# An encoder block whose experts' weights stream from memory: 1 MB parts in 16 recurring slots, in place of 2 MB halves in 8 recurring and 3 single-use slots

## The chip, the cores and the metric

The program runs on one core of one Trainium2 chip. The core has TensorE (PE; its weight loads are shown as PEld), VectorE (DVE), ScalarE (ACT), GpSimd (POOL) and SyncE (SP), and 16 DMA engines that move data between the chip's memory and SBUF. TensorE writes its products into the eight banks of PSUM. The metric is the device time of one execution in microseconds (us); lower is better.

## The reference

One encoder layer for x of 512 tokens by 1024 features, float32:

```python
h = rms_norm(x, norm1_g)                       # input projection, two attention branches, gates
x = x + einsum(gate_a * ya + gate_b * yb, w_out)
x = x + expert_choice_swiglu(rms_norm(x, norm2_g), w_router, w_gate, w_up, w_down)
return rms_norm(x, normf_g)

def expert_choice_swiglu(h, w_router, w_gate, w_up, w_down):
    aff = softmax(h @ w_router)                # 16 experts
    g, idx = top_k(aff.T, cap)                 # each expert takes its cap = 64 best tokens
    xin = h[idx]
    y = (silu(xin @ w_gate) * (xin @ w_up)) @ w_down * g
    return zeros.at[idx].add(y)
```

Each expert has three matrices of 1024 by 1024, 4 MB each: 16 experts have 192 MB, and each byte of them is read once.

## The kernel before, in words

The 512 tokens lie as four tiles of 128 (index c). The attention, the gates and the output projection come first. Then each tile's x2 is turned and multiplied with the router matrix, while the last output projections still run on TensorE; VectorE finds each expert's 64 tokens in eight rounds of "the best eight, then strike them out" (L1628, L1631), counts them (`count`), and forms `pos`, each token's place in its expert. `keep_clock` puts unused products on TensorE where it waits.

From `pos` a 0/1 matrix picks tokens. The experts go in eight pairs. For a pair, `gather` multiplies `pick` with the normalised rows of x2, held as a high part `xn_hi` and the rest `xn_lo` (both in the format fp32r), which gives the 2 x 64 chosen rows; `turn_xin` turns them so that features are on partitions, and VectorE applies the gain norm2_g (`xinT`). `gate_up(p, e)` multiplies them with the gate and up matrices of expert e of pair p. ScalarE applies the sigmoid, VectorE the two products (`activate`), `turn_act` turns the result into `actT`, and `down(p)` multiplies it with the down matrices. `y_hi` and `y_lo` are y times the token's affinity in two parts; `scatter` brings them back to the tokens through `give`, the turned `pick`, in four pieces between the products of the next pair's first expert, and VectorE adds them to x2 (`add`). After the last pair comes the final norm. Before the last down products TensorE copies x2 of three tiles into PSUM (L1338), to which the last pieces are added.

The first pair is gathered another way, since its xn parts are not there yet: `pick_first` holds the picks times the norm factor, and `gather_first` multiplies x2 itself with it, in full fp32 (which TensorE runs as two rows per product in the trace), so that the result is already turned. Its second half stands between the first expert's products. The parts `xn_hi` and `xn_lo` are made inside pair 0, once the slots whose memory they take are used.

The weights come through SyncE's queue in halves of 2 MB, 12 a pair: gate and up of expert 0 (h = 0, 1), of expert 1, and then the down halves in the order (h 0: e 0, e 1), (h 1: e 0, e 1). `slot_of` gives the slot: eight slots recur, and halves 3, 4 and 7 have a slot of their own that is used once. Eleven halves are loaded before the first gate product, some during the gates and the output projection, the last four after it. Then each load waits until the half that held its slot is used (`w_slot_used`); the first two of them are cut in two parts (`w_part_used`). The queue is in order. Engines work through their own programs in order too, and wait on semaphores.

## Time and profile before

| | us |
|---|---|
| median of three runs (lowest, highest) | 939.11 (937.24, 940.04) |
| the profiled execution, its own time | 939.72 |
| its span, from the first to the last instruction | 937.9 |
| busy: TensorE products, weight loads | 880.4, 564.7 |
| busy: VectorE, ScalarE, GpSimd | 350.2, 246.9, 21.8 |

In the profile "busy" is the time in which at least one instruction of the engine was running. A product of 128x512 in fp32 is two rows of the table, each 596 ns long and overlapping its neighbours. "DMA share" is the mean busy share of the 16 DMA engines; it can read a little above 1. "[0.75 <-PE psum L1109]" means that the engine was idle for 0.75 us before the instruction, and that this wait was ended by TensorE's line 1109.

### The profile page before, as it was taken

What the parts mean: (1) busy time and instruction counts of PE and PEld (TensorE: products, weight loads), DVE (VectorE), ACT (ScalarE), POOL (GpSimd) and SP (SyncE); (2) the same over time, 40 slices, a digit from 0 to 9 for tenths busy, and PEclk for the clock granted to TensorE, in tenths of its full rate; (3) what the DMA queues carried; (4) which work ended last, traced back from release to release, by engine and by line L of the source; (5) the groups of instructions that cost most, each with busy time, mean ns of one, the idle gap of its engine ahead of it and who ended that gap; (6) DMA issues with size and microseconds to landing.
All of it is one profiled execution on the core that took longest, in us unless ns stands there. A gap on an engine that the chain in (4) does not pass through costs nothing.

```text
span 937.9 us, 11252 instructions
## 1 busy us (share of the span) xinstructions
PE 880.4 (94%) x4730; PEld 564.7 (60%) x4730; DVE 350.2 (37%) x606; ACT 246.9 (26%) x445; POOL 21.8 (2%) x42
## 2 busy tenths in 40 slices
PE   5999899799989999899999999999998998989985
PEld 5999766578768888899954343343433434334332
DVE  4368676665714434333613221213121121221203
ACT  4433766665633322222002001010100101001002
POOL 1040000000000000000000000000000000000001
PEclk7999999999999999999999999999999999999999
DMA  8433111302127623772665899999999999999992
GB/s 262 96 91 90 45 45 46 112 18 63 51 71 226 196 80 106 266 273 88 273 237 211 346 428 428 427 427 429 427 427 426 430 428 426 430 427 426 428 419 101
DMA packets 77921, 239.78 MB, mean 256 GB/s; under 512 B 7728, under 2 KB 63152, under 8 KB 65072
## 3 DMA queue, kind: packets, MB, share of 16 engines
q1 hardware_dynamic: 72304, 235.94, 63.9%
q10 hardware_dynamic: 5568, 3.13, 1.2%
q8 instruction: 38, 0.62, 0.3%
q14 instruction: 11, 0.09, 0.0%
HBM read 236.96 MB, written 2.10 MB: 255 GB/s over the span
## 4 chain that ended last, share of the span: by engine, by line
PE 77%; DMA 16%; DVE 3%; ACT 2%; issue 1%; POOL 0%; SPq 0%; DVEq 0%; ACTq 0%
PE psum L1238 18%; DMA wslot<-in_w_down 14%; PE psum L863 10%; PE psum L865 10%; PE psum L864 10%; PE psum L1272 9%; PE psum L1292 3%; PE psum L1000 2%; PE psum L1012 2%; PE psum L1187 2%; PE psum L1199 2%; PE psum L869 2%; DMA w_raw<-in_w_in 1%; PE psum L970 1%; PE psum L986 1%
## 5 line engine op out<-in xcount | busy, mean ns | idle before, releaser
L1238 PE MATMUL psum<-wslot,xinT 128*64 128x512 f32 x1024 | 230.5, 596 | 11.5 <-DMA wslot<-in_w_up 6.1
L1238 PEld LDWEIGHTS psum<-wslot,xinT 128*64 128x64 f32 x1024 | 71.5, 137 | 152.5 <-issue 138.2
L1272 PE MATMUL psum<-wslot,actT 128*64 128x512 f32 x512 | 112.6, 594 | 7.7 <-DMA wslot<-in_w_down 7.7
L1379 DVE TENSOR_TENSOR w_lo<-w_raw,w_hi 128x1024 fp32r<-128x1024 f32 (+1 forms) x56 | 65.1, 1185 | 74.7 <-ACT w_hi L575 74.3
L863 PE MATMUL psum<-hT_hi,w_hi 128*128 128x512 f32 x224 | 88.9, 397 | 1.4 <-DVE qB_next L1477 1.4
L865 PE MATMUL psum<-hT_hi,w_lo 128*128 128x512 f32 x224 | 87.5, 391 | 0.0
L864 PE MATMUL psum<-hT_lo,w_hi 128*128 128x512 f32 x224 | 87.4, 390 | 0.0
L1272 PEld LDWEIGHTS psum<-wslot,actT 128*64 128x64 f32 x512 | 37.7, 137 | 77.5 <-issue 76.3
L813 ACT ACTIVATE act<-psum 128x512 f32<-128x512 f32 x16 | 9.6, 597 | 234.2 <-PE psum L1238 234.2
L575 ACT ACTIVATE w_hi<-w_raw 128x1024 fp32r<-128x1024 f32 (+1 forms) x56 | 55.7, 1021 | 26.0 <-DMA w_raw<-in_w_out 12.4
L1710 DVE TENSOR_TENSOR x<-x,psum 128x512 f32<-128x512 f32 x56 | 36.0, 684 | 67.5 <-PE psum L1292 67.5
L1694 DVE SCALAR_TENSOR_TENSOR y_lo<-psum,slot_aff,y_hi 128x512 fp32r<-128x512 f32 x16 | 11.3, 746 | 126.7 <-ACT y_hi L828 126.7
L863 PE MATMUL psum<-w_hi,hT_hi 128*128 128x256 f32 x192 | 55.8, 291 | 2.2 <-DVE w_lo L1379 2.2
L864 PE MATMUL psum<-w_lo,hT_hi 128*128 128x256 f32 x192 | 55.4, 288 | 0.0
L865 PE MATMUL psum<-w_hi,hT_lo 128*128 128x256 f32 x192 | 55.4, 288 | 0.0
L863 PEld LDWEIGHTS psum<-hT_hi,w_hi 128*128 128x128 f32 x224 | 42.1, 188 | 12.1 <-issue 3.9
L865 PEld LDWEIGHTS psum<-hT_hi,w_lo 128*128 128x128 f32 x224 | 42.1, 188 | 9.1
L864 PEld LDWEIGHTS psum<-hT_lo,w_hi 128*128 128x128 f32 x224 | 42.1, 188 | 8.3
L828 ACT ACTIVATE y_hi<-psum,slot_aff 128x512 fp32r<-128x512 f32 x16 | 10.1, 685 | 127.7 <-PE psum L1272 127.7
L1685 DVE TENSOR_TENSOR act<-act,psum 128x512 f32<-128x512 f32 x16 | 10.9, 684 | 86.0 <-ACT act L813 86.0
L863 PEld LDWEIGHTS psum<-w_hi,hT_hi 128*128 128x128 f32 x192 | 37.9, 197 | 2.6 <-issue 2.6
L863 PE MATMUL psum<-w_hi,mT_hi 128*128 128x256 f32 x128 | 36.7, 287 | 2.5 <-DVE x L1564 1.5
(190 smaller groups left out, 1260.1 us busy)
## 6 DMA issues: line engine op xcount, KB each, us to landing
wslot<-in_w_up SPq DMA_DIRECT2D x32, 2048.0 KB, 28.7
wslot<-in_w_gate SPq DMA_DIRECT2D x31, 2048.0 KB, 26.4
wslot<-in_w_down SPq DMA_DIRECT2D x31, 2048.0 KB, 32.7
w_raw<-in_w_in SPq DMA_DIRECT2D x40, 512.0 KB, 4.6
w_raw<-in_w_out SPq DMA_DIRECT2D x8, 512.0 KB, 8.0
x_in<-in_x SPq DMA_DIRECT2D x4, 512.0 KB, 10.3
w_raw<-in_w_o_a SPq DMA_DIRECT2D x8, 256.0 KB, 2.8
x<-in_x SPq DMA_DIRECT2D x1, 2048.0 KB, 7.9
```

The source lines that it names most:

```text
L575: act_.activation(hi, raw, ACT.Copy).then_inc(w_hi_done, 1)
L863: pe.matmul(out_, s_hi, m_hi, start=(k == 0), stop=False)
L864: pe.matmul(out_, s_hi, m_lo, start=False, stop=False)
L865: return pe.matmul(out_, s_lo, m_hi, start=False, stop=(k == n_k - 1))
L869: pe.matmul(into[:, 0:P], ident[:, :], ident[:, :], start=True, stop=True)
L1000: t = pe.transpose(tp[(0, 3)[u % 2]][:, P * k:P * k + P], probs_of(u)[:, P * k:P * k + P], ident[:, :])
L1012: mm = pe.matmul(tp[2][HD * hh:HD * hh + HD, :], vA[:, k, HD * kv:HD * kv + HD], pT[:, hh, k, :], start=(k == 0), stop=(k == NT - 1))
L1238: mm = pe.matmul(bank[2 * e + n][CAP * f:CAP * f + CAP, :], xinT[:, HALF * h + k, CAP * e:CAP * e + CAP], wslot[slot][:, k, SEQ * f:SEQ * ...
L1272: mm = pe.matmul(bank[4 + f][CAP * e:CAP * e + CAP, :], actT[:, e, k, CAP * h:CAP * h + CAP], wslot[slot][:, k, SEQ * f:SEQ * f + SEQ], st ...
L1292: mm = pe.matmul(bank[6 + f][:, :], give[:, p % 2, P * c:P * c + P], part[:, SEQ * f:SEQ * f + SEQ], start=(part is y_hi), stop=(part is y ...
L1379: dve.tensor_tensor(lo, raw, hi.bitcast(F32), ALU.subtract).then_inc(w_split, 1)
L1710: dve.tensor_tensor(part, part, bank[6 + f][:, :], ALU.add).then_inc(added, 1)
```

## The change

- Slots. Every half is now two parts of 1 MB (half of each partition's 16 KB). Part m goes to slot m mod 16; no slot is used once. 16 parts are loaded before the first gate product. The memory of the slots that recurred first (W0 and W0 + 16) now holds `xn_hi`, `xn_lo`, and at the end `fin`.
- Order of the down halves. By expert: (e 0: h 0, 1), (e 1: h 0, 1). `down(p, e, between)` is called once per expert; its products alternate over the two halves f of the columns in bank 4 + e, where before they alternated over the experts in bank 4 + f.
- Between the two down products stand `gather_slots` and both `gather` of the next pair, and the turns stand between the products (`between`). Scatter pieces come after steps 4, 7, 10, 13 instead of 3, 6, 9, 12.
- High and low rows. `high_xn` (ScalarE) and `low_xn` (VectorE, in two halves of the features) stand between the routing steps. They read x2 with a step of four elements and write it in the turned order, so that `turn_xin` reads it without a step.
- First gather. It uses `pick` and the xn parts like the others: features 0 to 511 before the first gate product, in two pieces of 256 columns, ScalarE's copy, two turns each, VectorE's gain; features 512 to 1023 after the first part's products.
- Affinity. It is multiplied in `activate` (the second product has a scalar operand now) and no longer in `high_y` and `low_y`, which work on one expert's 64 partitions at a time.

The core of the diff:

```diff
+++ after.py
@@ -60,9 +60,7 @@
 COL_GA = COL_BV + B_W
 COL_GB = COL_GA + D
 RING = 4
-SLOTS = 8
-AHEAD = 11
-PARTED = 2
+SLOTS = 16
 SCALE = HD ** -0.5
 SLOPES = [2.0 ** (-8.0 * (i + 1) / B_HEADS) for i in range(B_HEADS)]
 
@@ -154,11 +152,12 @@
 
 
     HALF = KC // 2
-    wslot = [sb(f"wslot{i}", [HALF, D], kib) for i, kib in
-             enumerate((W0, W0 + 16, W0 + 32, 0, 16, W0 + 48, 32, 64, W0 + 64, W0 + 80, 48))]
-
-    xn_hi = sb("xn_hi", [NT, D], W0 + 64, F32R)
-    xn_lo = sb("xn_lo", [NT, D], W0 + 80, F32R)
+    PART = HALF // 2
+    wslot = [sb(f"wslot{i}", [PART, D], kib + 8 * (i % 2)) for i, kib in
+             enumerate(at_ for at_ in (W0 + 32, 0, 16, W0 + 48, 32, 64, W0 + 64, W0 + 80) for _ in range(2))]
+
...
         y_hi_done = sem("y_hi_done")
@@ -335,26 +331,19 @@
 
 
         HALVES = [(w, h, e) for e in range(2) for h in range(2) for w in (w_gate, w_up)]
-        HALVES += [(w_down, h, e) for h in range(2) for e in range(2)]
+        HALVES += [(w_down, h, e) for e in range(2) for h in range(2)]
         PAIRS = NE // 2
-
-        def half_at(p, matrix, h, e):
-            return len(HALVES) * p + HALVES.index((matrix, h, e))
-
-        ONCE = {3: SLOTS, 4: SLOTS + 1, 7: SLOTS + 2}
-        recurring = [m for m in range(len(HALVES) * PAIRS) if m not in ONCE]
-
-        def slot_of(m):
-
-            return (ONCE[m], 0) if m in ONCE else divmod(recurring.index(m), SLOTS)[::-1]
-
-        def wait_half_used(eng, m):
-            slot, turn = slot_of(m)
-            eng.wait_ge(w_slot_used[slot], turn + 1)
-
-        def wait_half_in(eng, m):
-            slot, turn = slot_of(m)
-            eng.wait_ge(w_slot_in[slot], 16 * (turn + 1 + (turn > 0 and slot < PARTED)))
+        N_PARTS = 2 * len(HALVES) * PAIRS
+
+        def part_at(p, matrix, h, e, k):
+
+            return 2 * (len(HALVES) * p + HALVES.index((matrix, h, e))) + k // PART
+
+        def wait_part_used(eng, m):
+            eng.wait_ge(w_slot_used[m % SLOTS], m // SLOTS + 1)
+
+        def wait_part_in(eng, m):
+            eng.wait_ge(w_slot_in[m % SLOTS], 16 * (m // SLOTS + 1))
 
 
...
@@ -449,22 +436,20 @@
                     col = {"a": COL_A, "v": COL_BV, "ga": COL_GA, "gb": COL_GB}[s[0]] + P * s[1]
                 sp.dma_start(raw, w_in_k[:, :, col:col + P]).then_inc(done, 16)
 
-            def load_half(m):
-
-                p, entry = divmod(m, len(HALVES))
+            def load_part(m):
+
+                p, entry = divmod(m // 2, len(HALVES))
                 matrix, h, e = HALVES[entry]
                 rows = matrix[0, 2 * p + e].rearrange("(h p k) n -> h p (k n)", h=2, p=P)[h]
-                slot = slot_of(m)[0]
-                whole = wslot[slot][:, :, :].rearrange("p k n -> p (k n)")
-                if m in range(AHEAD, AHEAD + PARTED):
-
-                    part = HALF * D // 2
-                    sp.wait_ge(w_part_used[slot], 1)
-                    sp.dma_start(whole[:, 0:part], rows[:, 0:part]).then_inc(w_slot_in[slot], 16)
-                    wait_half_used(sp, recurring[recurring.index(m) - SLOTS])
-                    sp.dma_start(whole[:, part:], rows[:, part:]).then_inc(w_slot_in[slot], 16)
-                    return
-                sp.dma_start(whole, rows).then_inc(w_slot_in[slot], 16)
+                n = PART * D
+                if m >= SLOTS:
+                    wait_part_used(sp, m - SLOTS)
+                sp.dma_start(wslot[m % SLOTS][:, :, :].rearrange("p k n -> p (k n)"),
+                             rows[:, n * (m % 2):n * (m % 2) + n]).then_inc(w_slot_in[m % SLOTS], 16)
+
+            def load_half(m):
...
             for n in range(len(strips)):
@@ -474,32 +459,28 @@
                 if n == 1:
                     for c in range(2, NT):
                         load_x(c)
-                if strips[n] in (("wo", 2), ("wo", 3), ("wo", 4)):
+                if strips[n] == ("wo", 2):
 
                     sp.wait_ge(pv_done, OA + OB)
-                    load_half(strips[n][1] - 2)
+                    load_half(0)
                 if strips[n] == ("out", 3):
 
                     sp.wait_ge(branch_done, 2 * KC)
                     sp.dma_start(x2[:, :, :], x_t).then_inc(x_again_in, 16)
 
                     sp.wait_ge(proj_done, g_at[("gate", KC - 1, 1)] + 1)
-                    load_half(5)
+                    load_half(1)
                 if strips[n] == ("out", 5):
-                    load_half(6)
+                    load_half(2)
 
             sp.wait_ge(m_lo_done, KC)
-            load_half(8)
+            load_half(3)
 
             wait_split(sp, len(strips) - 1)
-            load_half(9)
+            load_half(4)
             sp.wait_ge(proj_done, len(groups))
-            for m in (3, 4, 7, 10):
-                load_half(m)
-            for m in range(AHEAD, len(HALVES) * PAIRS):
-                if m >= AHEAD + PARTED:
-                    wait_half_used(sp, recurring[recurring.index(m) - SLOTS])
-                load_half(m)
+            for m in range(10, N_PARTS):
+                load_part(m)
             for n in range(2 * NT):
                 c, f = LAST_TILES[n // 2], n % 2
...
                 cols = slice(SEQ * f, SEQ * f + SEQ)
@@ -786,28 +767,37 @@
                 act_.activation(logit[:, c, :], logit[:, c, :], ACT.Exp,
                                 accum_out=ssum[:, c:c + 1]).then_inc(sexp_done, 1)
 
-            for step, c in ((square_tile, 0), (square_tile, 1), (read_h2, 0), (read_h2, 1), (square_tile, 2),
-                            (route_exp, 0), (read_h2, 2), (route_exp, 1), (read_h2, 3), (square_most, 3),
-                            (route_exp, 2), (square_rest, 3), (route_exp, 3)):
+            def high_xn(c):
+                act_.wait_ge(rstd2, c + 1)
+                act_.activation(xn_hi[:, c, :].rearrange("p (h k i) -> p h k i", h=2, k=HALF),
+                                x2[:, c, :].rearrange("p (h i k) -> p h k i", h=2, k=HALF), ACT.Copy,
+                                scale=rstd[:, c:c + 1]).then_inc(xn_hi_done, 1)
+
+            for step, c in ((square_tile, 0), (square_tile, 1), (read_h2, 0), (read_h2, 1), (high_xn, 0),
+                            (square_tile, 2), (route_exp, 0), (read_h2, 2), (route_exp, 1), (high_xn, 1),
+                            (read_h2, 3), (square_most, 3), (route_exp, 2), (high_xn, 2), (square_rest, 3),
+                            (route_exp, 3), (high_xn, 3)):
...
+            def gather_first(c, n):
+
+                cols = slice(2 * P * n, 2 * P * n + 2 * P)
+                for part in (xn_hi, xn_lo):
+                    mm = pe.matmul(bank[6 + n][:, 0:2 * P], pick[:, c, :, :], part[:, c, cols],
+                                   start=(c == 0 and part is xn_hi), stop=(c == NT - 1 and part is xn_lo))
+                if c == NT - 1:
+                    mm.then_inc(gathered, 1)
...
-            def down(p):
-
-                pe.wait_ge(actT_done, 2 * p + 2)
+            def down(p, e, between):
+
+                pe.wait_ge(actT_done, 2 * p + e + 1)
...
                 for h in range(2):
-                    halves = [half_at(p, w_down, h, e) for e in range(2)]
-                    for m in halves:
-                        wait_half_in(pe, m)
                     for k in range(HALF):
+                        m = part_at(p, w_down, h, e, k)
+                        if k % PART == 0:
+                            wait_part_in(pe, m)
                         for f in range(2):
-                            for e in range(2):
-                                slot = slot_of(halves[e])[0]
-                                mm = pe.matmul(bank[4 + f][CAP * e:CAP * e + CAP, :],
-                                               actT[:, e, k, CAP * h:CAP * h + CAP],
-                                               wslot[slot][:, k, SEQ * f:SEQ * f + SEQ],
-                                               start=(h == 0 and k == 0), stop=(h == 1 and k == HALF - 1))
...
+                            mm = pe.matmul(bank[4 + e][CAP * f:CAP * f + CAP, :],
+                                           actT[:, e, k, CAP * h:CAP * h + CAP],
+                                           wslot[m % SLOTS][:, k % PART, SEQ * f:SEQ * f + SEQ],
+                                           start=(h == 0 and k == 0), stop=(h == 1 and k == HALF - 1))
+                        if k % PART == PART - 1:
+                            mm.then_inc(w_slot_used[m % SLOTS], 1)
+                        between(HALF * h + k)
...
+            def low_xn(c, h):
+
+                dve.wait_ge(xn_hi_done, c + 1)
+                cols = slice(SEQ * h, SEQ * h + SEQ)
+                dve.scalar_tensor_tensor(xn_lo[:, c, cols].rearrange("p (k i) -> p k i", k=HALF),
+                                         x2[:, c, cols].rearrange("p (i k) -> p k i", k=HALF), rstd[:, c:c + 1],
+                                         xn_hi[:, c, cols].rearrange("p (k i) -> p k i", k=HALF).bitcast(F32),
+                                         ALU.mult, ALU.subtract).then_inc(xn_lo_done, 1)
...
             read_h2(1)
             route_max(0)
             add_residual(3, 2)
+            low_xn(0, 0)
+            low_xn(0, 1)
             read_h2(2)
```

TensorE's order before, from the first gather to the third half (wslot_102 is slot 0, wslot_103 slot 1, wslot_104 slot 2):

```order
L1187 MATMUL psum<-pick_first,x_89 128x128 [waits pick_first_done]
L1187 MATMUL psum<-pick_first,x_89 128x128 x3
L869 MATMUL psum<-ident 128x128
L1238 MATMUL psum<-wslot_102,xinT 64x512 [waits xin_done,w_slot_in0]
L1238 MATMUL psum<-wslot_103,xinT 64x512 [waits w_slot_in1]
L1238 MATMUL psum<-wslot_103,xinT 64x512 x3
L1187 MATMUL psum<-pick_first,x_89 128x128 x16
L1238 MATMUL psum<-wslot_103,xinT 64x512 x4
L1179 MATMUL psum<-aff,pick 128x2 [waits pick_done]
L1238 MATMUL psum<-wslot_104,xinT 64x512 [waits w_slot_in2,xin_done]
```

and after the change, at the same place:

```order
L1175 MATMUL psum<-xn_hi,pick 128x256 [waits pick_done,xn_lo_done]
L1175 MATMUL psum<-xn_lo,pick 128x256
L1184 MATMUL psum<-ident,xin_next 128x128 [waits xin_read]
L1236 MATMUL psum<-wslot_102,xinT 64x512 [waits xin_done,w_slot_in0]
L1236 MATMUL psum<-wslot_102,xinT 64x512 x3
L1198 MATMUL psum<-xn_hi,pick 128x512 [waits xn_lo_done,xin_read]
L1198 MATMUL psum<-xn_lo,pick 128x512
L1236 MATMUL psum<-wslot_103,xinT 64x512 [waits xin_done,w_slot_in1]
L1206 MATMUL psum<-ident,xin_next 128x128 [waits xin_read]
L1236 MATMUL psum<-wslot_104,xinT 64x512 [waits w_slot_in2]
```

The two gathers on pick_first (16 products each) are replaced by 16 products of 256 columns ahead of the gates and 8 of 512 columns behind the first part's four; a turn by TensorE of the copied rows is added to both.

TensorE's order after the change from the last part of the first down product to that of the second, in pair 0 (in the kernel before, the same gather and turns stand in a row ahead of `down`):

```order
L1266 MATMUL psum<-wslot_105,actT 64x512 [waits w_slot_in3]
L1167 MATMUL psum<-aff,pick 128x2 [waits act_done,pick_done]
L1198 MATMUL psum<-xn_hi,pick 128x512
L1198 MATMUL psum<-xn_lo,pick 128x512
L1266 MATMUL psum<-wslot_106,actT 64x512 [waits w_slot_in4,slot_aff_done,actT_done]
L1206 MATMUL psum<-ident,xin_next 128x128 [waits xin_read]
L1266 MATMUL psum<-wslot_107,actT 64x512 [waits w_slot_in5]
L1266 MATMUL psum<-wslot_108,actT 64x512 [waits w_slot_in6]
L1206 MATMUL psum<-ident,xin_next 128x128 [waits xin_read]
L1266 MATMUL psum<-wslot_109,actT 64x512 [waits w_slot_in7]
L1212 MATMUL psum<-ident,pick 128x128 x4
```

The gather of the next pair moved from before the down products to between them, and its turns to between the products of the second.

VectorE's order at the end of the routing, before:

```order
L1564 TENSOR_TENSOR x_89<-x_89,psum 128x256 [waits proj_done]
L1587 RECIPROCAL small<-small 128x1 [waits sexp_done]
L1588 TENSOR_SCALAR aff<-logit,small 128x16 [waits dve_step]
L1572 COPY h2T<-psum 128x256 [waits x2_turned]
L1579 TENSOR_REDUCE small<-psum 128x1 [waits logits_done]
```

and after:

```order
L1587 TENSOR_TENSOR x_89<-x_89,psum 128x256 [waits proj_done]
L1610 RECIPROCAL small<-small 128x1 [waits sexp_done]
L1611 TENSOR_SCALAR aff<-logit,small 128x16 [waits dve_step]
L1619 SCALAR_TENSOR_TENSOR xn_lo<-x_89,small,xn_hi 128x512 [waits xn_hi_done]
L1595 COPY h2T<-psum 128x256 [waits x2_turned]
L1619 SCALAR_TENSOR_TENSOR xn_lo<-x_89,small,xn_hi 128x512 [waits xn_hi_done]
L1602 TENSOR_REDUCE small<-psum 128x1 [waits logits_done]
```

One half-width subtraction stands ahead of each of the two reads on which TensorE's last router product, and the choice of tokens, wait.

## Rows read from the trace of the kernel before

**Rows 1.** The page: GB/s moved in 40 slices of 23.4 us

```profile
GB/s 262 96 91 90 45 45 46 112 18 63 51 71 226 196 80 106 266 273 88 273 237 211 346 428 428 427 427 429 427 427 426 430 428 426 430 427 426 428 419 101
```

**Rows 2.** Windows: us, busy PE, PEld, DVE, ACT, POOL, clock, DMA share, GB/s

```profile
441.00:460.50 19.50, 19.14 (x148) 17.87 (x148) 15.55 (x38) 1.82 (x4) 0.23 (x1) 1.00 0.98 415
460.50:521.00 60.50, 60.50 (x292) 34.19 (x293) 14.56 (x25) 7.74 (x10) 0.00 (x0) 1.00 0.49 180
521.00:913.00 392.00, 373.04 (x1718) 153.69 (x1716) 81.84 (x134) 32.14 (x54) 0.00 (x0) 1.00 1.01 427
```

**Rows 3.** Chain of waits: start us, length us, engine, tile, line, count

```profile
459.65 7.74 PE psum L1187 x32
...
472.91 7.66 PE psum L1187 x32
...
705.41 33.04 DMA wslot<-in_w_down
...
764.56 33.30 DMA wslot<-in_w_down
...
917.15 7.11 PE psum L1272 x32
924.28 0.69 ACT y_hi L828
```

**Rows 4.** Windows: one expert pair, and two stretches of 1 MB loads

```profile
541.79:595.38 53.59, 53.59 (x254) 22.31 (x256) 12.11 (x21) 4.75 (x8) 0.00 (x0) 1.00 1.01 428
...
473.00:477.00 4.00, 4.00 (x18) 4.00 (x18) 0.00 (x0) 0.00 (x0) 0.00 (x0) 1.00 0.94 344
477.00:479.00 2.00, 2.00 (x10) 2.00 (x10) 0.00 (x0) 0.00 (x0) 0.00 (x0) 1.00 1.00 422
```

**Rows 5.** Timeline of SyncE's queue: start us, us of the issue, line, transfer

```profile
469.52 0.33 SPq L463 DMA_DIRECT2D wslot<-in_w_down  x1
471.24 0.33 SPq L465 DMA_DIRECT2D wslot<-in_w_down  x1
472.95 0.33 SPq L463 DMA_DIRECT2D wslot<-in_w_gate  x1
...
518.85 0.33 SPq L467 DMA_DIRECT2D wslot<-in_w_gate  x1
```

**Rows 6.** Tile wslot: issue to landing of the loads at 469.52, 471.24, 472.95

```profile
DMA to landing us min/median/max: 5.3/5.3/5.3
...
DMA to landing us min/median/max: 7.2/7.2/7.2
...
DMA to landing us min/median/max: 8.0/8.0/8.0
```

**Rows 7.** Timeline: start us, us, engine, line, operation, before it idle

```profile
413.81 0.28 PE L863 MATMUL psum<-w_hi,mT_hi 128*128 128x256 f32 x1
...
413.93 0.28 PE L864 MATMUL psum<-w_lo,mT_hi 128*128 128x256 f32 x1
...
459.06 1.87 DVE L1647 TENSOR_SCALAR pick_first<-slot_id,pos,small 128x64 f32<-128x64 f32 x8
...
467.54 5.37 PE L1238 MATMUL psum<-wslot,xinT 128*64 128x512 f32 x24
```

**Rows 8.** Timeline and groups by line: operations of the kinds that the change adds

```profile
440.07 0.42 PE L1109 MATMUL psum<-ident,x 128*128 128x128 f32 x2
...
440.52 0.43 DVE L1572 COPY h2T<-psum 128x256 f32<-128x256 f32 x1 [0.75 <-PE psum L1109]
...
L802 ACT ACTIVATE xin_next<-psum 128x512 f32<-128x512 f32 x14 | 8.4, 598 | 53.2 <-PE psum L1199 53.2
...
L1701 DVE SCALAR_TENSOR_TENSOR xn_lo<-x,small,xn_hi 128x1024 fp32r<-128x1024 f32 x4 | 4.9, 1278 | 2.7 <-PE psum L1238 2.7
...
L1338 PE MATMUL psum<-x,ident 128*128 128x512 f32 x12 | 5.4, 598 | 0.8 <-ACT actT L817 0.8
```

More of the change, by code:

```diff
@@ L1612, in _ @@
             add_residual(2, 3)
+            low_xn(1, 0)
+            low_xn(1, 1)
             read_h2(3, NT, HALF, KC - 2)
@@ L1637, in _ @@
                 .then_inc(counted, 1)
+            low_xn(3, 0)
             dve.wait_ge(taken_copied, 1)
@@ L1726, in _ @@
                 activate(2 * p)
-                if p == 0:
-                    wait_half_used(dve, 4)
-                    for c in range(NT):
-                        low_xn(c)
                 activate(2 * p + 1)
-                if p == 0:
-                    read_give(0, bank[4])
-                    read_slots(0, bank[5])
+                low_y(p, 0)
                 if p + 1 < PAIRS:
```

271 lines of the change are left out of this document (142 added, 129 removed).

## The prediction

> **What bounds the kernel now.** I read the slices of the whole span first [rows 1]: to slice 22 the DMA engines move what the layer happens to need, and from slice 24 to slice 39 they stand at 426 to 430 GB/s without a gap. That stretch is the expert stage, 192 pieces of 1 MB (201 MB, by 1.049 each) of weights. The windows say the same in three numbers [rows 2]: the engines are full from 441.0 to 460.5 us, at a share of 0.49 from 460.5 to 521, at 1.01 from 521 to 913. So at the end the transfers bound the kernel, and what can still be moved is when their unbroken stream begins, plus what follows the last one.
>
> The chain of waits shows the two ends [rows 3]. At 459.65 TensorE is on the chain with a gather of 7.74 us before the first expert, then again with one of 7.66 us inside it. From 705.41 the chain is a transfer, 33 us a pair, and from pair to pair 59.15 us pass (705.41 to 764.56). A pair that does not wait takes 53.59 us, all of it TensorE [rows 4]. TensorE is thus the faster of the two by 5.6 us a pair, and lives on the weights loaded ahead until 700 us.
>
> Why did the stream not begin at 467.5, when the first expert starts? Eleven 2 MB halves are in, all slots are full, and the program loads again only as slots come free. Three of the eleven are used once, and their memory goes to xn_hi, xn_lo and to the tiles of y and give, so their use frees nothing for the stream. The queue's own rows [rows 5]: issues at 469.52, 471.24, 472.95, and after several idle stretches the one at 518.85, from which on it never runs dry. By then 11 + 5 halves have been issued; 80 halves, 160 MB-parts, are left, and the last of them releases TensorE at 917.15 [rows 3]. That is (917.15 - 518.85) / 160 = 2.489 us a part, start and one small gain load included. The stretch 460.5 to 521 wasted half of its 60.5 us, some 31 us of transfer; but it began with 11 halves loaded.
>
> **The change, part by part.**
>
> 1. Ring. All 16 parts recur, none is used once. Eight halves are in at the start instead of eleven: 3 more to load behind it, 6 x 2.489 = +14.9 us. Against that the release of part 1 loads at once part 17, and so on. TensorE uses a part in 1.72 us (issue to issue, 469.52 to 471.24 [rows 5]), the engines bring one in 2.49, so each part used adds 0.77 us of queued work, and the pieces in between take it away: after the first part the gather of the second half of the features (8 products of 512 columns, 1.9 us at twice the 0.12 us of a 256-column one below) leaves a gap of 1.1 us (part 1 is free at 1.7, part 2 at 5.3; the transfer of part 1 runs from 3.9 to 6.4, that of part 2 can start at 7.5). Then the work queued is 0.6 us at part 5, 8 us after the second expert's gates, and 52.0 - 41.8 = 10 us at the end of the first down product, before the 4.8 us pause in which the next pair is gathered. It does not run dry again. For the shallow start I add one row's worth: of the three 1 MB loads issued one behind the other the first lands 5.3, the second 7.2, the third 8.0 us after issue [rows 6], so landings at 474.8, 478.4, 480.95, gaps of 3.6 and 2.5 us. One gap of 3.6 instead of 2.49 is 1.1 us. Bounds for the start: 0 and 2 x 1.1 more, value 1.1 + 1.1 = 2.2 us.
>
> 2. First gather. Before, 16 products of full fp32 in two passes (32 rows) take 7.74 us, then DVE scales; the gates start at 467.54, that is 8.48 us after the first pick at 459.06 [rows 7]. Now: pick tile one 0.3, semaphore and start 0.3 (0.59 us in the row before), 16 products of 256 columns, 0.12 us apart (413.81 to 413.93, products of the same width, also of high and low parts [rows 7]) = 1.9 us, ScalarE reads 256 columns, 0.4 (a 512-column read is 0.598 [rows 8]), two turns 0.42 and DVE 0.43, both seen at this size [rows 8], hops 0.3. Sum 4.05 us: the gates start near 463.1, 4.4 us earlier. Bounds: 3 us of saving (each hop twice), 5.5.
>
> 3. High and low rows while routing. Four reads on ScalarE of 1.1 us and eight half-width DVE operations of 0.64 us (half of 1.278 [rows 8]). They stand in front of instructions that wait for TensorE. The tightest is low_xn(2, 0) before the read at 440.52, with 0.75 us idle before it [rows 8]: 0.64 fits; the one at the count sits in a wait for the turned count, and the last behind the picks. Cost 0; if the reads with a step of four elements ran at half speed, 0.6 us late there and as much at the next, so 0 to 1.2 us late. ScalarE has no such neighbour. What is removed, 4.3 + 4.9 us of the same work inside the first pair, was beside TensorE and gave nothing.
>
> 4. Pair. The matrix work is the same: the down product alternates banks by half of the columns, not by expert. gather_slots, gather and the turns move, none is added beyond pair 0. Each wait they carry was issued for earlier: the turned activations of the second expert come 3.4 us after its gates, the next input is read while the second down product runs. I leave 53.6 us a pair [rows 4]. Eight pairs from 463.1 end near 892; the stream ends at 905, so TensorE has 13 us to spare, and what it does in a pair decides nothing. If cover is gone, 13 us of new waits in all are free, beyond that each costs itself. On DVE and ScalarE, low_y and high_y are twice as many with half the partitions, 2 x 1.4 us more a pair in waits of tens of us.
>
> 5. Tail. The last landing is followed by 7.11 us of products now [rows 3], both experts' last halves. In the new order the last four parts are one expert's. The sums of the old x, 12 rows in 5.4 us [rows 8], come before them: the part before lands 9.96 us ahead of the end, is used by -8.2, the sums end at -2.8, three parts take it to +2.3, the last to +4.1. So 3.0 us less. From the first y_hi at 924.28 to 937.9 nothing changes, 13.6 us.
>
> **Sum.** First release: 463.1 + 1.72 + 0.26 (467.54 + 1.72 to 469.52) = 465.1. 176 parts x 2.489 = 438.1, plus 2.2: last landing 905.4, against 917.15. Last product 909.5 against 924.26, so the span is 937.9 - 14.7 = 923.2. The profiled execution reported 939.72, 1.8 above its span and 0.6 above the median of the three runs; I predict 923.2 + 1.8 - 0.6 = 924.4 us.
>
> The parts are 8 KB a partition, the halves were 16 KB; nearly all traffic of the stage before is 16 KB, so the 2.489 is carried over. Where loads of 8 KB ran alone the windows show both: 344 GB/s at a share of 0.94 from 473 to 477, 422 at 1.00 from 477 to 479 [rows 4]. I take the second, since it is a queue with its load already started, as the steady stream is; the first would be 3.05 us a part.
>
> The Trainium skill, "DMA: Bandwidth & Descriptors", section "Bandwidth", speaks against the change: it tells of 341 GB/s for a 1 MB transfer and 425 for one of 16 MB, and asks for batches. Its figures are for transfers issued from another engine; by 341 in every part, an estimate from that page, the stream would take 541 us instead of 438 and the kernel 1027. The first window agrees with it, the second and the unbroken 427 of 2 MB loads do not.
>
> **Rivals.**
> - *A fixed cost shows behind each of 176 transfers.* A lone 1 MB load lands after 5.3 us, 2.8 more than its share of the stream. If one twentieth of that, 0.14 us, is not hidden, 25 us are lost: 949 us, slower than before. It decides from 14.7 / 176 = 0.084 us a part. For it: the 3.6 us gap and the first window. Against: in the deep queue the next transfer's start lies under the one before, and the gap behind it was 2.5. The Trainium skill's rule above would come out on this side.
> - *The stream runs dry during the first two pairs.* The lead there is 1 to 10 us, and a pause I have misplaced (the gather pause of 4.8 us with a late wait behind it) empties it. If twice 4 us go, 932. For it: the share of 0.49 in this stretch before [rows 2]. Against: those gaps come from three slots that do not recur and from a gather of 7.66 us.
> - *Routing or the first gather is no shorter.* If DVE's added work delays the routing by 1.2 and the hops take all of 4.4, the result is 924.4 + 5.6 = 930.
> - *TensorE becomes the bound.* New waits of over 1.7 us a pair use up 13 us; with 2.5 a pair it ends at 931 (8 x 2.5 less 13 is 7 us late). For it: 12 more waits on slots per pair. Against: a landed part costs no time.
>
> **How the numbers follow.** Forecast 0.62 (920 to 928), fixed cost a part 0.11 in all (0.03 of it under the 0.084 and still faster), dry stream 0.13, no shorter start 0.08, TensorE 0.06. What a measurement tells from no change is 0.3%, 2.8 us, so faster means under 936.3. The forecast, the last three rivals and the small end of the first are on that side, less some 0.07 where they add up: faster 0.85, same 0.06, slower 0.09. The range 918 to 937 holds the forecast and the mild rivals; above it lies the fixed cost, below it a start with no loss at all (2.2 less) and a faster gather.
>
> **What would show it.** Right: gates begin near 463; the DMA share is 1.0 from about 470 on without an idle stretch; consecutive parts land 2.45 to 2.5 us apart; last landing near 905 with about 4 us of products behind it. The low-row operations end before the reads they precede. Wrong: a share of 1.0 at under 415 GB/s (rival one), idle DMA between 470 and 560 (two), a gate start after 466 (three), or a stream with gaps late in the stage while TensorE never waits (four).

## The result, and the profile after

| | before | after |
|---|---|---|
| median of six runs each on one chip (lowest, highest) | 939.4 (937.24, 940.04) | 931.46 (930.04, 934.08) |
| ratio after to before, 95% interval | | 0.9921 [0.9903, 0.9940] |
| the profiled execution, its own time; its span | 939.72; 937.9 | 930.23; 928.4 |
| busy: TensorE products; VectorE; ScalarE | 880.4; 350.2; 246.9 | 880.2; 366.4; 261.8 |

The kernel is faster by 0.8%, 7 us; forecast were 14.7. The time lies in the range, on the far side of the forecast's own 920 to 928.

The page after, GB/s in 40 slices of 23.2 us (it answers [rows 1]):

```profile
GB/s 265 98 92 91 46 46 47 114 17 64 54 69 139 103 84 108 243 302 60 217 360 421 421 422 420 421 422 422 419 422 422 421 421 421 421 421 421 422 420 134
```

The unbroken stream begins two slices earlier, as forecast. But it stands at 421 where it stood at 427 to 428. The windows after (us, busy PE, PEld, DVE, ACT, POOL, clock, DMA share, GB/s), for [rows 2]:

```profile
460.00:521.00 61.00, 60.66 (x288) 24.70 (x288) 11.69 (x24) 8.14 (x14) 0.00 (x0) 1.00 0.93 371
...
540.00:640.00 100.00, 100.00 (x462) 40.03 (x460) 24.34 (x43) 11.31 (x19) 0.00 (x0) 1.00 1.01 421
640.00:880.00 240.00, 233.77 (x1056) 89.42 (x1052) 58.91 (x101) 24.41 (x41) 0.00 (x0) 1.00 1.01 421
```

The first window has a share of 0.93 where [rows 2] had 0.49. In the others the share is 1.01, as it was at 427 GB/s: the engines are as full as ever and move 1.5% less. Ahead of the stream, the starts of the first issue (SyncE's queue) and of the first gate products (TensorE):

```profile
461.13 1.94 PE L1236 MATMUL psum<-wslot,xinT 128*64 128x512 f32 x8 [0.33 <-DVE xinT L1698]
```

```profile
463.09 11.27 SPq L447 DMA_DIRECT2D wslot<-in_w_down  x5
```

And the chain at its end, for [rows 3]:

```profile
872.59 27.87 DMA wslot<-in_w_down
900.50 1.94 PE psum L1266 x8
902.44 5.35 PE psum L1361 x12
907.79 7.04 PE psum L1266 x32
```

The last part is issued at 883.75 and lands 26.6 us later, at 910.35. The last product ends at 914.83, 4.5 us behind it, where [rows 3] showed 7.1.

**What the clock at the start adds.** The absolute times mislead by 3 us. Both kernels do the same until the output projection, yet its first weight load is issued at 204.24 before and at 201.34 after:

```profile
204.24 0.37 SPq L438 DMA_DIRECT2D w_raw<-in_w_o_a  x1
```

```profile
201.34 0.37 SPq L425 DMA_DIRECT2D w_raw<-in_w_o_a  x1
```

At 20 to 22 us TensorE was granted 0.50 of its clock (1.2 GHz) in the one execution and 0.87 on average in the other; which it is changes from execution to execution: in the thirteen profiles of this study the issue lies at 203.6 to 204.2 where this clock was 0.50, and at 200.7 to 201.3 where it was 0.84 or more. So I count from this issue:

| from the first load of w_o_a, us | before | after | difference | forecast |
|---|---|---|---|---|
| first ring load issued | 265.3 | 261.8 | -3.5 | -4.4 |
| from there to the last landing | 447.6 | 447.3 | -0.4 | -7.3 |
| from there to the end of the span | 20.8 | 18.1 | -2.7 | -3.0 |
| together | | | -6.6 | -14.7 |

The -6.6 lie in the ratio's interval, which is 5.6 to 9.1 us less. Almost the whole miss is in the middle row. It splits so: the fourth part lands at 479.0 (issued 471.2, 7.8 later), and 172 more until 910.35, 2.508 us each. Before, the load issued at 518.85 landed at 527.55, and 158 parts followed until 917.15, 2.466 us each. That is 0.042 x 172 = 7.2 us. The first four parts took 15.9 us, 6.0 more than four at 2.466.

**A second fall of the clock.** Between 439 and 449 us, at the end of the router products, where TensorE has just been idle for about a microsecond (in the profiles without the fall too), the granted clock fell to 0.50 for some three to seven microseconds in five of the profiles of the experiments below (late start, pause in the middle, sums ahead, later gather, 64 neighbouring partitions), and stayed at 1.00 in all others. Counted from w_o_a the first gather starts at 256.4 to 256.7 in the six profiles with the new VectorE reads and a full clock, and at 257.8 to 258.9 in those five. So a first release that is up to 2.6 us later need not come from an experiment's edit.

### The profile page after: what moved, and what is told of

Read it like the earlier page. It is cut to its first block, busy times and chain, and to the rows that moved or that the text cites. A ratio compares the mean times of both kernels' runs of the same rounds, so it can differ in the third digit from the quotient of the medians.

```text
span 928.4 us, 11338 instructions
## 1 busy us (share of the span) xinstructions
PE 880.2 (95%) x4698; PEld 544.6 (59%) x4698; DVE 366.4 (39%) x635; ACT 261.8 (28%) x464; POOL 23.8 (3%) x42
## 4 chain that ended last, share of the span: by engine, by line
PE 67%; SPq 19%; DMA 5%; DVE 4%; ACT 2%; issue 1%; POOL 1%; DVEq 0%; ACTq 0%; POOLq 0%
SPq L447 19%; PE psum L1236 13%; PE psum L851 10%; PE psum L852 10%; PE psum L853 10%; PE psum L1266 7%; DMA wslot<-in_w_down 3%; PE psum L988 2%; PE psum L1198 2%; PE psum L1287 2%; PE psum L1000 2%; PE psum L857 1%; DMA w_raw<-in_w_in 1%; PE psum L958 1%; PE psum L974 1%
## 5 line engine op out<-in xcount | busy, mean ns | idle before, releaser
L1236 PEld LDWEIGHTS psum<-wslot,xinT 128*64 128x64 f32 x1024 | 68.9, 136 | 144.1 <-issue 126.3
L1266 PE MATMUL psum<-wslot,actT 128*64 128x512 f32 x512 | 120.9, 601 | 4.7 <-DMA wslot<-in_w_down 4.7
L1266 PEld LDWEIGHTS psum<-wslot,actT 128*64 128x64 f32 x512 | 32.9, 136 | 66.9 <-issue 57.9
L1738 DVE TENSOR_TENSOR y_lo<-psum,y_hi 64x512 fp32r<-64x512 f32 x32 | 22.0, 689 | 84.8 <-ACT y_hi L817 84.3
L807 ACT ACTIVATE actT<-psum 128x512 f32<-128x512 f32 x16 | 9.6, 597 | 151.4 <-PE psum L1248 151.4
L817 ACT ACTIVATE y_hi<-psum 64x512 fp32r<-64x512 f32 x32 | 18.9, 592 | 80.6 <-PE psum L1266 80.2
```

Of the source, the lines that this page charges most:

```text
L817: act_.activation(y_hi[CAP * e:CAP * e + CAP, SEQ * f:SEQ * f + SEQ], bank[4 + e][CAP * f:CAP * f + CAP, :], ACT.Copy).then_inc(y_hi_done, 1)
L1236: mm = pe.matmul(bank[2 * e + n][CAP * f:CAP * f + CAP, :], xinT[:, HALF * h + k, CAP * e:CAP * e + CAP], wslot[m % SLOTS][:, k % PART, SE ...
L1266: mm = pe.matmul(bank[4 + e][CAP * f:CAP * f + CAP, :], actT[:, e, k, CAP * h:CAP * h + CAP], wslot[m % SLOTS][:, k % PART, SEQ * f:SEQ * ...
L1738: dve.tensor_tensor(y_lo[rows, cols], bank[4 + e][CAP * f:CAP * f + CAP, :], y_hi[rows, cols].bitcast(F32), ALU.subtract).then_inc(y_lo_do ...
```

## The experiments

Each was timed beside the kernel before; its ratio compares with the changed kernel's 0.9921. "Counted from w_o_a" means less the start of that issue. The changed kernel's own numbers are 261.8 for the first issue and 727.1 for the end of the span. "..." in a diff marks lines left out.

**Loads of 2 MB in the new ring.** All behind the first 16 parts:

```diff
+            def load_whole(half):
...
+                for m in (2 * half, 2 * half + 1):
+                    wait_part_used(sp, m - SLOTS)
+                sp.dma_start(whole[half % (SLOTS // 2)][:, :, :].rearrange("p k n -> p (k n)"), rows)\
...
```

> The changed kernel, but behind the first 16 parts every load is one transfer of a whole 2 MB half (16 KB a partition) into two neighbouring slots, as soon as both are used. Theory (each row of a transfer costs a DMA engine a fixed 9 ns beside its bytes: 613 ns for 16 KB at 427.5 GB/s, 311 ns for 8 KB at 421.3): the share-1.0 windows return to 427 to 428 GB/s, 6.4 us are won on 176 MB-parts, and 2 to 3 us are lost at the start, since the first release comes after two parts and the gather between them; 927 to 929 us against 931.5. Rival (what was lost is in the shallow start and in SyncE's 2.1 us a transfer, not in the rate): windows stay at 421 GB/s, and the later first release makes it 2 to 3 us slower than the changed kernel, 934.

931.5 us, ratio 0.9924 [0.9906, 0.9942]. The window and the queue of this kernel:

```profile
640.00:880.00 240.00, 234.09 (x1063) 91.24 (x1062) 59.76 (x102) 24.41 (x41) 0.00 (x0) 1.00 1.01 428
```

```profile
467.92 4.48 SPq L499 DMA_DIRECT2D whole<-in_w_down  x2
```

428 GB/s are back, so the slower stream belongs to the parts. But the first load waits for two parts and for the gather between them: 265.8 counted from w_o_a, 4 us later than in the changed kernel (its clock at 440 to 450 us was full). The expected total of 927 to 929 is not in the median. In the profiled execution the span counted from w_o_a is 724.2 against 727.1, 2.9 us less: the first release is 4.1 us later, from there to the last landing (873.2 + 33.1 = 906.3) it takes 438.4 instead of 447.3, and what follows is 2.0 longer. The ratios, each good to 1.7 us, neither show nor exclude that gain. What is shown is the rate, and that the later release takes back much of it.

**Parts of 1 MB as 64 partitions of 16 KB**, to tell the number of transfers from the length of the rows:

```diff
+                for j in range(2):
+                    part = slice(P // 2 * j, P // 2 * j + P // 2)
+                    sp.dma_start(whole[half % (SLOTS // 2)][part, :, :].rearrange("p k n -> p (k n)"), rows[part, :])\
...
```

> As the previous one, but each 2 MB half comes as two transfers of 1 MB with 64 partitions each, so the rows are 16 KB and the number of transfers is that of the changed kernel. Theory (the cost is in the rows): 427 to 428 GB/s in the steady windows and the time of the whole-half kernel within 1.5 us, 927 to 929. Rival (the cost is in the number of transfers, 0.08 us each): 421 GB/s, 6 us more than the whole-half kernel, 934 or so.

1347.2 us, ratio 1.437 [1.434, 1.440]; neither theory. Its window:

```profile
530.00:880.00 350.00, 218.74 (x756) 80.27 (x756) 42.40 (x72) 17.86 (x30) 0.00 (x0) 0.83 1.01 216
```

Half the rate at a full share: the engines are busy, but a transfer into 64 neighbouring partitions takes twice its time. The kernel says nothing of the disputed cost; the same edit with other partitions does.

**Parts of 1 MB as every second partition, 16 KB each:**

```diff
-                    part = slice(P // 2 * j, P // 2 * j + P // 2)
+                    part = slice(j, P, 2)
```

> As the kernel with two transfers of 64 partitions per half, but the first transfer takes the even partitions and the second the odd ones. 16 KB rows, 1 MB and as many transfers as the changed kernel. That one ran at 216 GB/s. Theory (rows set the rate, and the halving came from writing into one half of the partitions at a time): 427 GB/s again, and the time of the kernel with whole halves, 931.5. Rival (a transfer of 64 rows of 16 KB is slow by itself, or transfers cost a fixed time each): 216 GB/s and 1347 us, or 421 GB/s and 934 to 938.

930.59 us, ratio 0.9908 [0.9885, 0.9931], and

```profile
640.00:880.00 240.00, 233.44 (x1063) 92.25 (x1060) 59.06 (x101) 24.39 (x41) 0.00 (x0) 1.00 1.01 428
```

As many transfers of 1 MB as in the changed kernel, and 428 GB/s. So a transfer costs nothing that shows; it is the 8 KB rows. (This kernel starts late, like the one with 2 MB loads, with its first issue at 265.9 counted from w_o_a; its interval holds the changed kernel's ratio.) The half rate of the experiment above came from which partitions, not from their number.

**Rows of 4 KB.** The same parts, each partition's 8 KB as two pieces:

```diff
+    wslot = [w[:, j::2, :] for w in whole for j in range(2)]
...
+                             rows[:, n * (m % 2):n * (m % 2) + n].rearrange("p (k n) -> p k n", k=PART))\
```

> The changed kernel with 1 MB parts whose rows are 4 KB: each of the two features of a part's partition goes to another place of the slot pair, so a part is 256 rows. The number of transfers and bytes is unchanged. Theory (9 ns a row): 4096 B take 151 + 9 = 160 ns, 409.5 GB/s in the steady windows, 176 parts of 2.56 instead of 2.49 us, 12.6 us slower than the changed kernel: 944 us. Rival (number of transfers): 421 GB/s and 931.5 us.

943.1 us, ratio 1.0065 [1.0048, 1.0082]; theory, in rate and time:

```profile
530.00:880.00 350.00, 336.09 (x1516) 128.99 (x1514) 84.24 (x146) 35.72 (x60) 0.00 (x0) 1.00 1.03 409
```

428, 421 and 409 GB/s for rows of 16, 8 and 4 KB are 613, 311 and 160 ns a row on one of 16 engines: each row costs about 9 ns beside its bytes. The 4 KB rows read the same source bytes per transfer as the 8 KB rows, and the alternate partitions skip every second 16 KB of the source at 428 GB/s, so the gaps in what a transfer reads are not the cause. A row is a packet here. The pages of the kernel before and of the changed one say, for SyncE's queue:

```profile
q1 hardware_dynamic: 72304, 235.94, 63.9%
```

```profile
q1 hardware_dynamic: 85840, 235.95, 65.2%
```

These 13536 packets more are the 12032 rows more and 16 for each of the 94 transfers more. The Trainium skill ("DMA: Bandwidth & Descriptors", section "Why small descriptors are slow (HBM only)") tells of a fixed cost for each packet, which agrees in kind; the 9 ns are from these runs. The table of load streams of the Trainium skill (same page, section "iDMA fabric — 4 AXI ports for 8 engines, asymmetric across TPBs") has 408.7 GB/s for a load stream of 1 MB transfers with rows of 4 KB. The 409 here agree.

**A later first release.** 25 unused products ahead of the first gate in place of one:

```diff
-            keep_clock(1, bank[0])
+            keep_clock(25, bank[0])
```

> The changed kernel with 24 more unused products on TensorE (about 0.25 us each, 6.1 us) right before the turns of the first gather, so that the first gate product and the first release of a part come 6 us later. Theory (from the first release on the transfers never stop, so the end is that release plus 176 parts): the whole 6 us appear at the end, 937 to 938 us against 931.5. Rival (TensorE has slack of over 10 us in the stage and takes the delay up): under 1.5 us more.

938.13 us, ratio 0.9991 [0.9977, 1.0004]. The first issue:

```profile
469.48 4.24 SPq L447 DMA_DIRECT2D wslot<-in_w_down  x2
```

That is 268.3 counted from w_o_a, 6.6 us later than in the changed kernel: 5.1 by the products, 1.5 by the second fall of the clock. The median is 6.7 us longer, the span counted from w_o_a 6.3. Theory: the first release sets the end one for one.

**The same pause inside pair 4's gather:**

```diff
+                    if p == 4:
+                        pe.wait_ge(y_lo_done, 4 * p)
+                        keep_clock(24, bank[5])
```

> The changed kernel with the same 6 us of unused products once in the middle of the stage, between the two down products of pair 4. Theory (there TensorE is ahead of the transfers by enough queued loads, and its delay decides nothing): 931.5 us, within 1 us of the changed kernel. Rival (TensorE, or its lead over the queue, still bounds the first pairs, and each pause adds up): 4 to 6 us more, 936 to 937.

933.74 us, ratio 0.9941 [0.9921, 0.9961], against 0.9921 [0.9903, 0.9940]. The pause stands at 731.91 us in the chain, 5.36 us long, and the stream stays at 421 across it:

```profile
731.91 5.36 PE psum L857 x48
```

```profile
640.00:880.00 240.00, 238.41 (x1107) 96.64 (x1108) 60.89 (x104) 24.39 (x41) 0.00 (x0) 1.00 1.01 421
```

The median is 2 us higher, and the intervals overlap. The trace puts even these down to something else: in the profiled execution the first issue is already 2.6 us late (264.3 counted from w_o_a) by the second fall of the clock, and from there to the end of the span it is 464.5 us against 465.3 in the changed kernel. TensorE's time in the middle is worth nothing that shows.

**The sums of the old x (x2 of three tiles, copied into PSUM) between the products of the last pair's first down product**, and no longer behind it:

```diff
+                    if p == PAIRS - 1 and step in (1, 5):
+                        copy_sum((3, 0)[step // 5])
+                    if p == PAIRS - 1 and step == 7:
+                        pe.wait_ge(actT_done, 2 * p + 2)
+                        copy_sum(1)
```

> The changed kernel, but the 12 rows that copy x2 into the sums (5.4 us) stand between the products of the last pair's first down product instead of between the two down products. Theory (the stream sets the end, and what counts is TensorE's work behind the last landing, 4.5 us now, 1.9 when nothing is queued): last product 1.9 to 2.2 us behind the last landing, 2.5 us faster, 929 us. Rival (TensorE has too little room in the first down product, 4 parts arriving in 10 us with 6.9 us of products, and the sums push the rest back all the same): within 0.5 us of the changed kernel, 931.5.

931.95 us, ratio 0.9934 [0.9917, 0.9950]: no gain. The chain shows the rival:

```profile
893.95 1.94 PE psum L1266 x8
895.88 1.91 PE psum L1304 x4
...
907.91 7.04 PE psum L1266 x32
```

From 893.95 to the last product TensorE works without a break. A sum (L1304) put there pushes everything back; it would have to lie where TensorE waits for a landing.

**The same, spread further ahead** (one behind step 3 and one behind step 9 of the last gates, the third as above):

> The changed kernel with the sums of the old x for tiles 3, 0 and 1 moved ahead: tile 3's behind step 3 and tile 0's behind step 9 of the last gates, tile 1's behind step 7 of the next to last down product. Theory (the last four parts land 2.5 us apart, TensorE uses one in 1.8, and what stands between is the 5.4 us of sums, of which some 2.6 are in the way): work behind the last landing 1.9 to 2.3 us instead of 4.5, ratio to the changed kernel 0.9975, about 929. Rival (TensorE's work from the release of the last gates on is unbroken, so a product moved ahead only shifts another back, as when all sums stood before the last down products): 931.5.

931.59 us, ratio 0.9922 [0.9900, 0.9943]: no gain in the medians. In the trace the edit works:

```profile
903.94 5.60 PE L1266 MATMUL psum<-wslot,actT 128*64 128x512 f32 x24
910.05 1.94 PE L1266 MATMUL psum<-wslot,actT 128*64 128x512 f32 x8 [0.52 <-DMA wslot<-in_w_down]
```

TensorE waits for the last part, issued at 883.40 and landed 26.61 us later; the last product ends 2.0 us behind it (4.5 in the changed kernel), and the span counted from w_o_a is 724.0 against 727.1. Six runs from 927.4 to 933.2 neither show nor exclude 2.5 us.

**The second gather two steps later:**

```diff
-                    if step == 1:
+                    if step == 3:
                         gather(0, 1)
-                    if step == 3:
+                    if step == 5:
                         turn_xin(0, 1)
```

> The changed kernel with the gather of the second half of the features behind step 3 of the first gates instead of step 1, and the next one's turn moved behind step 5. Theory (first releases set the end): part 2 comes free 1.9 us earlier, the second and third gap of the start shrink, 0.5 to 1 us less: 930.5 to 931. Rival (the gather only moves the same gap one part back): 931.5, no change.

930.69 us, ratio 0.9918 [0.9903, 0.9933]: what either side expects lies inside the interval. Here the chain's last wait for a landing ends at 876.66 + 27.88 = 904.54, after a first issue at 467.40: 437.1 us, against 900.46 - 463.09 = 437.4. That is 0.3 us gained in one execution of each kernel, near the rival and short of the 0.5 to 1 of the theory.

**High and low rows in their natural order**, the step of four elements read by TensorE in the gather, and no longer by ScalarE and VectorE (one of the four places that change):

```diff
-                        mm = pe.matmul(bank[6 + f][:, :], pick[:, c, :, :], part[:, c, cols],
+                        mm = pe.matmul(bank[6 + f][:, :], pick[:, c, :, :],
+                                       part[:, c, cols].rearrange("p (i k) -> p k i", k=HALF),
```

> The changed kernel, but the high and low rows keep x2's order, so ScalarE and VectorE read without a step, and the step of four elements moves into the moving operand of the gathers on TensorE. Theory (the stepped read doubled VectorE's low-row operations from 0.64 to 1.14 us and pushed the end of the routing back by about a microsecond, and TensorE reads such an operand at full speed): the first release 1 to 1.5 us earlier and 930 to 930.5 us. Rival (TensorE pays for the step: its gather products take longer, 16 of them ahead of the gates): the first release as late or later, 931.5 to 933.

946.08 us, ratio 1.0072 [1.0055, 1.0089]. In the lines grouped by shape, first this kernel, then the changed one:

```profile
L1197 PE MATMUL psum<-xn_hi,pick 128*128 128x512 f32 x60 | 38.9, 648 | 0.0
```

```profile
L1198 PE MATMUL psum<-xn_hi,pick 128*128 128x512 f32 x60 | 24.2, 403 | 0.0
```

The chain of this kernel, and then of the changed one, from gather to gather:

```profile
742.95 7.46 PE psum L1197 x16
...
801.75 7.46 PE psum L1197 x16
```

```profile
558.25 3.78 PE psum L1198 x16
...
613.36 3.77 PE psum L1198 x16
```

Sixteen products take 7.46 instead of 3.78 us and a pair 58.80 instead of 55.11. With 8 pairs behind a first release at 465.85 TensorE itself ends last, as the window shows (240.00 us busy of 240), while the stream still moves 421:

```profile
640.00:880.00 240.00, 240.00 (x1034) 90.06 (x1032) 57.98 (x99) 24.96 (x42) 0.00 (x0) 1.00 1.01 421
```

The rival's mechanism, and dearer than it said. This is the fourth rival of the prediction made real, by work and not by waits. The theory's other half is right: without the step VectorE's subtractions are shorter, and the choice of tokens (the first MAX8) begins earlier:

```profile
440.25 0.74 DVE L1619 SCALAR_TENSOR_TENSOR xn_lo<-x,small,xn_hi 128x512 fp32r<-128x512 f32 x1
443.38 0.69 DVE L1665 MAX8 best<-psum 16x8 f32<-16x512 f32 x1 [1.00 <-PE psum L1139]
```

Counted from w_o_a (203.69 here) the choice begins at 239.7. Before it was 239.8 (444.00 less 204.24), in the changed kernel 240.9. But the first gather takes 3.8 instead of 2.0 us, so the first release, 262.2, comes no earlier.

**Small at the start, large after it.** 1 MB parts for halves 8 to 11 and for the last one, 2 MB loads between, with the later gather and the spread sums:

```diff
+        def is_whole(half):
+            return 12 <= half < 95
...
```

> The changed kernel with halves 12 to 94 loaded whole again (2 MB, 16 KB a row), halves 8 to 11 and the last one in 1 MB parts as in the changed kernel, the second gather two steps later and the sums of the old x for tiles 3, 0 and 1 made among the last expert's products. Theory (rows of 8 KB cost 0.04 us a part, and the first release sets the end): the first release stays near 463 to 464, the window from 640 to 880 shows 427 to 428 GB/s instead of 421, and 2 x 83 parts x 0.04 = 6.4 us less stream; the sums give another 2 and the later gather 0.7; less some 0.5 to 2 for the coarser releases of the first whole loads: 922 to 925. Rival (whole loads need two parts free at once, and the start loses about as much as the rows give, as in the kernel with all loads whole, 931.5): 928 to 930, of which the sums give the 2.

926.29 us (922.51 to 926.67), ratio 0.9865 [0.9845, 0.9885], which does not touch the changed kernel's interval: the fastest kernel of the study, 1.35% below the one before. The median is 1.3 us above what theory gave and clear of the rival.

```profile
463.06 11.28 SPq L458 DMA_DIRECT2D whole<-in_w_down  x5
```

```profile
640.00:880.00 240.00, 237.05 (x1070) 92.60 (x1068) 58.88 (x101) 24.78 (x42) 0.00 (x0) 0.99 1.01 428
```

The first issue is where the changed kernel has it (261.9 from w_o_a). The last part is issued at 870.88 and lands 33.2 us later, at 904.1: 441.0 us behind the first issue instead of 447.3. These 6.2 us are what theory gave for the rows (6.4). The chain ends so:

```profile
894.37 3.65 PE psum L1289 x16
898.03 1.91 PE psum L1327 x4
899.94 7.04 PE psum L1289 x32
```

From 894.37 on it is TensorE alone. The last product ends at 906.98, 2.9 us behind the last landing (4.5 in the changed kernel). The span counted from w_o_a is 719.5 against 727.1, 7.5 us less; the ratios differ by 5.3. Three edits are changed at once here; the rows' share is read from the stream, and the shares of the sums and of the gather are not told apart.

## Why the prediction was right and wrong

- *First release.* Forecast 465.1, read 463.1; but 2.9 us of that came from the clock at the start. Counted from w_o_a it is 3.5 us earlier than before, of 4.4 forecast. The first gather gave its 4.4: from its first product to the first issue it was 9.87 us and is 5.40. It starts 0.9 us later. The cost that I set at nothing has the size of the bound beside it: the subtractions on VectorE took 1.1 us, not 0.64, as with the stepped reads at half speed. In the timeline of VectorE after:

```profile
437.42 1.13 DVE L1619 SCALAR_TENSOR_TENSOR xn_lo<-x,small,xn_hi 128x512 fp32r<-128x512 f32 x1 [0.71 <-ACT xn_hi L772]
...
438.78 1.14 DVE L1619 SCALAR_TENSOR_TENSOR xn_lo<-x,small,xn_hi 128x512 fp32r<-128x512 f32 x1
442.19 0.69 DVE L1666 MAX8 best<-psum 16x8 f32<-16x512 f32 x1 [0.70 <-PE psum L1140]
```

  That these cause the missing 0.9 us is shown by the kernel with rows in natural order: with subtractions of 0.74 us the choice of tokens begins at 239.7 us from w_o_a, as before, and with those of 1.13 at 240.9 to 241.2 in six profiles at full clock.
- *The step that failed: "so the 2.489 is carried over".* The average of the loads with 16 KB rows was taken for parts with 8 KB rows, and it was not a rate: 158 parts in steady flow took 2.466 each, and the rest was the 8.7 us landing of the first load, spread over 160 parts. In the changed kernel 172 parts took 2.508 each. So a start was counted as rate, and the true cost of a part was missed by 0.042. Over 172 parts that is 7.2 us, the whole miss of the stream. The steady windows give 0.038 of it (a part of 1.049 MB takes 2.491 us at 421 GB/s, 2.453 at 427.5), 6.5 us, near the 6.2 that the stream won back with long rows after the start; the rest lies outside of these windows.
- *The same miss, booked otherwise.* As a number 2.489 happens to be what a part with 8 KB rows costs. Whoever takes 176 x 2.49 as the stream's rate finds 9 us for its start and end, where the forecast had 2.2. In either booking the fault is the average, which held start and rate together; that the number fits the new rate is chance.
- *The sign that was in the text.* The window with 422 GB/s [rows 4] fits what a full queue of 8 KB rows does (421). But it could not have settled it: in the kernel before, 9 us in which only 2 MB loads with 16 KB rows were under way also read 422. Only long windows tell 421 from 427.

```profile
500.00:509.00 9.00, 9.00 (x47) 5.18 (x44) 2.51 (x7) 1.68 (x3) 0.00 (x0) 1.00 1.00 422
```

- *Loss at the start.* By the first booking the forecast held 2.2 + 176 x 0.023 = 6.2 us for the start; 6.0 were measured. Right, but 4.0 of it stood there unplanned, inside the 2.489: luck.
- *Rival one* had the right place and sign: something behind each part that is not hidden. It was put down to the transfer; the kernel with alternate partitions shows that it is the row. At 0.042 us a part it stayed at half of the 0.084 from which it decides, so the change remains a gain.
- *Rival two* (a dry stream) did not occur: a share of 0.93 in the first window and 1.01 behind it. *Rival three* is true in one half: VectorE's added work delays the choice of tokens by 1.1 us, near the 1.2 it named. The first gather is shorter by what was forecast, so the gates still start 3.5 us earlier.
- *Rival four.* A pair takes TensorE 55.1 us, 1.5 more than the 53.6 carried over, close to the 1.7 at which it decides. No wait was added; 1.0 of the 1.5 is in the down products, whose 64 rows took 13.95 us in one run before and take 15.0 in six runs with turns between them. The prediction had set this at nothing, since "the matrix work is the same". TensorE did not decide, because the stream is slower too; and the pause inside pair 4 shows room left. With the rows in natural order, 58.8 us a pair, it decides.
- *Tail.* 4.5 us of products behind the last landing, forecast 4.1; 13.6 behind them, as forecast.

## What to carry to other kernels

When a stream of loads bounds a stage, divide its cost into what is paid per row, per transfer and once at the start, and take each from its own rows: an average over the whole stream mixes them, and an edit changes one at a time. Split loads where a release is waited for (at the start, and at the very end), and keep them large, with long rows, where the queue is full. Before comparing absolute times of two profiles, find an instruction ahead of the first edit and count from it, and look at the granted clock between there and the place of the edit.

## What the runs showed of the hardware beyond that

- A transfer of 1 MB into 64 neighbouring partitions runs at 216 GB/s with all 16 engines at a share of 1.01; into every second partition at 428. The Trainium skill ("DMA: Bandwidth & Descriptors", section "Rules for kernel authors") advises against two transfers to disjoint halves of the partitions, which serialize, and for one to all 128. The trace agrees: 216 GB/s that way, 428 with whole loads.
- The length of SyncE's issues goes with the rows, not with the transfers or with how full the engines are. All of these streams have a share of 1.01 to 1.03. With rows of 8 KB an issue took 2.13 us in the median, with rows of 4 KB 2.36. With rows of 16 KB it took 0.33 in 2 MB loads and 0.5 in 1 MB parts on alternate partitions, though by the time to landing (29 us there, 27 in the changed kernel) as many parts were under way. The profile then puts 19% of the changed kernel's chain on SyncE's queue. No run shows that this costs time: the stream goes on at 421 GB/s under it. The last two issues of the changed kernel:

```profile
881.58 4.30 SPq L447 DMA_DIRECT2D wslot<-in_w_down  x2
```

- TensorE's products of 128x512 in fp32r took 648 ns with a step of four elements in the moving rows and 403 without; VectorE's subtraction took 1.1 us with the step and 0.7 without. A stepped read costs on either engine, so it belongs on the one with time to spare.
